# Four modulation chunks of the second layer moved between output projection tiles, attention scores handled map by map, and the order at the router changed

## What is computed

```python
def trunk_layer(x, cond, p, l, ctx_kv, ang):
    mod = cond @ p['w_mod'] + p['b_mod']                   # (1024) @ (1024, 6144)
    sh1, sc1, g1, sh2, sc2, g2 = jnp.split(mod[:, None, :], 6, axis=-1)
    h = rms_norm(x, p['g_pre_mix']) * (1.0 + sc1) + sh1
    y, k, v = mixer(h, p, l, ctx_kv, ang)                  # convolution, Hyena, differential attention, @ w_out
    x = x + g1 * rms_norm(y, p['g_post_mix'])
    h = rms_norm(x, p['g_pre_ffn']) * (1.0 + sc2) + sh2
    y = moe(h.reshape(B * L, D), p).reshape(B, L, D)       # sigmoid router, 64 experts, top 8, one shared expert
    return x + g2 * rms_norm(y, p['g_post_ffn']), k, v

    def block(qi):                                         # attention: two maps (c = 0, 1) for each head
        s = jnp.einsum('bhqcd,bhkcd->cbhqk', qi, k32) * scale
        pr = jax.nn.softmax(s, axis=-1)
        return jnp.einsum('bhqk,bhkd->bhqd', pr[0] - lam * pr[1], v32)
```

## Time and profile before

| | before |
|---|---|
| median of 3 runs | 1786.36 us (1785.29 to 1787.12) |
| the profiled execution | 1788.74 us, of which the span of the trace is 1786.9 us |
| mean granted TensorE clock | 0.974 |
| PE busy | 1687.2 us (94%) |
| DVE, ACT, POOL busy | 617.0 us (35%), 364.6 us (20%), 189.6 us (11%) |
| HBM read | 533.76 MB |

### The profile page before, as it was taken

How to read it: one execution, slowest core, us unless ns; L and a number is a source line. 1 busy time by engine, 2 the same in 40 slices (tenths; PEclk the granted TensorE clock), 3 DMA queues, 4 the chain that set the end, 5 groups by cost and what they waited for, 6 DMA issues and landing times.

```text
span 1786.9 us, 21952 instructions
## 1 busy us (share of the span) xinstructions
PE 1687.2 (94%) x8340; PEld 811.3 (45%) x8340; DVE 617.0 (35%) x1651; ACT 364.6 (20%) x820; POOL 189.6 (11%) x205
## 2 busy tenths in 40 slices
PE   4999889989999999999969998999999999999996
PEld 1555445544444444444435553555444444444442
DVE  2358362422222222222144674533222222222223
ACT  2110243211111111111141014431111111111111
POOL 0000000011111111111100000001111111111110
PEclk8999989999999999999979999899999999999998
DMA  9212690299999999999832138116799999999993
GB/s 402 97 78 94 244 378 2 70 381 368 418 401 412 417 392 415 420 419 419 350 130 94 63 127 335 54 47 275 307 414 419 397 421 392 411 419 420 419 420 134
DMA packets 77290, 530.50 MB, mean 297 GB/s; under 512 B 10881, under 2 KB 14081, under 8 KB 21633
## 3 DMA queue, kind: packets, MB, share of 16 engines
q1 hardware_dynamic: 67392, 503.90, 69.0%
q0 software_dynamic: 9792, 25.18, 3.6%
HBM read 533.76 MB, written 5.77 MB: 302 GB/s over the span
## 4 chain that ended last, share of the span: by engine, by line
PE 90%; DVE 4%; DMA 3%; ACT 2%; issue 1%; SPq 0%; ACTq 0%; POOL 0%; DVEq 0%
PE PSB L874 30%; PE PSB L883 15%; PE PSB L866 7%; PE PSB L861 6%; PE PSB L928 6%; PE PSB L929 5%; PE PSB L829 4%; PE PSB L916 4%; DMA RING<-in_wmod 3%; PE PSB L901 1%; PE PSB L649 1%; PE PSB L890 1%; PE PSB L781 1%; PE PSB L734 1%; PE PSB L719 1%
## 5 line engine op out<-in xcount | busy, mean ns | idle before, releaser
L874 PE MATMUL PSB<-WB,EX 128*32 128x512 f32 (+2 forms) x1408 | 431.9, 597 | 0.0
L874 PE MATMUL PSB<-RING,EX 128*32 128x512 f32 (+2 forms) x1344 | 417.1, 598 | 1.8 <-DVE EX L1667 1.8
L883 PE MATMUL PSB<-RING,AT 128*32 128x512 f32 (+2 forms) x720 | 229.9, 602 | 4.9 <-issue 3.8
L1685 DVE TENSOR_TENSOR YL<-PSB,YH 128x512 fp32r<-128x512 f32 x136 | 94.1, 692 | 357.2 <-ACT YH L1298 357.2
L883 PE MATMUL PSB<-WB,AT 128*32 128x512 f32 (+2 forms) x704 | 210.8, 596 | 0.0
L874 PEld LDWEIGHTS PSB<-WB,EX 128*32 128x32 f32 (+2 forms) x1408 | 113.3, 126 | 135.4 <-issue 135.3
L928 PE MATMUL PSB<-YH,SCAT 128*128 128x512 f32 x408 | 171.6, 421 | 2.8 <-DVE YL L1685 2.8
L537 POOL TENSOR_SCALAR SCAT<-CST,LSTT 128x384 fp32r<-128x384 f32 x68 | 84.9, 1249 | 836.6 <-PE PSB L929 836.4
L874 PEld LDWEIGHTS PSB<-RING,EX 128*32 128x32 f32 (+2 forms) x1344 | 105.8, 124 | 122.4 <-issue 122.4
L929 PE MATMUL PSB<-YL,SCAT 128*128 128x512 f32 x408 | 161.1, 395 | 0.0
L1667 DVE COPY EX<-PSB 128x512 f32<-128x512 f32 x68 | 47.0, 692 | 317.4 <-PE PSB L916 317.4
(11 more groups left out here) (265 smaller groups left out, 1708.5 us busy)
## 6 DMA issues: line engine op xcount, KB each, us to landing
RING<-in_exp_w_gate SPq DMA_DIRECT2D x64, 1024.0 KB, 12.5
RING<-in_exp_w_up SPq DMA_DIRECT2D x64, 1024.0 KB, 14.8
RING<-in_exp_w_down SPq DMA_DIRECT2D x64, 1024.0 KB, 13.3
WB<-in_exp_w_gate SPq DMA_DIRECT2D x64, 1024.0 KB, 10.3
WB<-in_exp_w_up SPq DMA_DIRECT2D x64, 1024.0 KB, 13.6
WB<-in_exp_w_down SPq DMA_DIRECT2D x64, 1024.0 KB, 13.5
RING<-in_wmod SPq DMA_DIRECT2D x16, 2048.0 KB, 10.6
KSYS<-in_wmod SPq DMA_DIRECT2D x8, 2048.0 KB, 11.5
```

The costliest lines, as they stand in the source:

```text
L874: mm = nc.tensor.matmul(PS[6][s0:s0 + w, :].rearrange("p (w f) -> p w f", w=2), e[:, k, s0:s0 + w], rawgu[n % NBUF][:, k], start=(k == 0), ...
L883: mm = nc.tensor.matmul(dst[s0:s0 + w, :], AT[:, j, s0:s0 + w], rawdn[n % NBUF][:, hf, j], start=(j == 0), stop=(j == 1))
L1685: v.tensor_tensor(YLb[s % 2][:, hf * 512:(hf + 1) * 512], PS[6 + hf][:, :], YHb[s % 2][:, hf * 512:(hf + 1) * 512].bitcast(F32), ALU.subtr ...
```

## The change

1. **Chunks 12 to 15** leave layer 0's attention. The attention loops of both layers now have the same filler (eight chunks, then pieces 0 to 6). Chunks 12 to 15 are multiplied between the `w_out` tiles, `mod_columns(2)` stands behind `router(0, 1)`; they use PS[4] and PS[5], and `to_features(l, 1, t)` takes the banks of its tile's `w_out` instead of PS[4] and PS[5]. SP issues chunks 12 to 15 behind the attention's loads, ACT's `mod_rows(2)` and `mod_column(2)` move along.
2. **Map by map:** the scores of each map signal and wait for themselves; DVE takes two reductions and two scalings where it took one each.
3. **At the router,** both layers: `shared_up(l, 0)` is cut in two halves with `to_features(l, 1, 2)` between them; ACT and DVE write the features of tile 2 ahead of the shared activations; DVE does `shared(l, 2)` ahead of the second list; `shared_down(l, 2, 0)` stands ahead of the wait for the third list.

```diff
...
         XNK = [x.rearrange("p t (q k) -> p t k q", k=KD) for x in XN]
-        FTB = ((0, 2, 4), (4, 4, 4))
+        FTB = ((0, 2, 4), (6, 0, 2))
+        ROWB = (6, 6, 4, 6)
+        COLB = (6, 5, 4, 5)
         YB = ((6, 0, 2), (0, 2, 4))
...
-            first, n = (4, 12) if l == 0 else (16, 8)
-            ended = {8: 1, 12: 2} if l == 0 else {8: 3}
-            return first + i if i < n else None, ended.get(i)
+            first = 4 if l == 0 else 16
+            return first + i if i < 8 else None, 2 * l + 1 if i == 8 else None
         def pieces(l, i):
-            if l == 0:
-                return range(0, 2) if i == 12 else range(2, 4) if i == 13 else range(0)
             return range(i - 9, i - 8) if 9 <= i < 12 else range(3, 5) if i == 12 else range(5, 7) if i == 13 else range(0)
...
                         weight_in(l, "o1")
+                if l == 0:
+                    for j in range(12, 16):
+                        mod_in(j)
                 sp.wait_ge(mod_used, 15 if l == 0 else 23)
...
-            def shared_up(l, t):
-
-                if t == 0:
+            def shared_up(l, t, first=0, last=KD):
+
+                if t == 0 and first == 0:
                     pe.wait_ge(gu_in[0], 32 * loads(l, 0))
-                for k in range(KD):
+                for k in range(first, last):
                     mm = gate_up(SHARED, HT[:, :, t * P:(t + 1) * P], k)
-                mm.then_inc(sh_gu, 1)
+                if last == KD:
+                    mm.then_inc(sh_gu, 1)
...
                 pe.wait_ge(d_sel, l + 1)
+                pe.wait_ge(a_col, 3)
                 for a in range(NT):
...
                 lists(l, 2)
+                shared_down(l, 2, 0)
                 pe.wait_ge(d_lst, LSTN * (NU * l + 3))
-                shared_down(l, 2, 0)
                 rows(l, 0, 0)
...
                         k0, kn = keys(t)
-                        if i >= 1:
-                            pe.wait_ge(a_exp, 2 * (NUN * l + i))
                         for c in range(2):
-                            mm = nc.tensor.matmul(PS[c][:, 0:kn * P],
-                                                  QT[c * DK:(c + 1) * DK, h, t * P:(t + 1) * P],
-                                                  KT[c * DK:(c + 1) * DK, h, k0:k0 + kn * P], start=True, stop=True)
-                        mm.then_inc(pe_S, 1)
+                            if i >= 1:
+                                pe.wait_ge(a_exp, 2 * (NUN * l + i - 1) + c + 1)
+                            nc.tensor.matmul(PS[c][:, 0:kn * P],
+                                             QT[c * DK:(c + 1) * DK, h, t * P:(t + 1) * P],
+                                             KT[c * DK:(c + 1) * DK, h, k0:k0 + kn * P], start=True, stop=True).then_inc(pe_S, 1)
                     if 1 <= i <= NUN:
...
                 gate_rows(l, 0, 0)
-                for p in range(4 if l == 0 else 7, 8):
+                for p in range(7, 8):
                     w_out_piece(l, p)
                 gate_rows(l, 0, 1)
                 pe.wait_ge(a_OT, NUN * (l + 1))
                 w_out(l, 1, 0)
+                if l == 0:
+                    mod_chunk(12)
                 w_out(l, 1, 1)
+                if l == 0:
+                    mod_chunk(13)
                 to_features(l, 1, 0)
                 pe.wait_ge(a_grow, 8 * l + 4)
                 w_out(l, 2, 0)
                 to_tokens(l, 0)
+                if l == 0:
+                    mod_chunk(14)
                 w_out(l, 2, 1)
+                if l == 0:
+                    mod_chunk(15)
                 to_features(l, 1, 1)
                 router(l, 0)
                 to_tokens(l, 1)
                 router(l, 1)
-                shared_up(l, 0)
+                if l == 0:
+                    mod_columns(2)
+                shared_up(l, 0, 0, 4)
                 to_features(l, 1, 2)
+                shared_up(l, 0, 4, KD)
                 router(l, 2)
...
                         kn = keys(units[i][0])[1]
-                        act.wait_ge(d_max, 2 * (NUN * l + i + 1))
                         if i >= 2:
                             act.wait_ge(d_P, K_P * l + 4 * (i - 1))
                         for c in range(2):
+                            act.wait_ge(d_max, 4 * (NUN * l + i) + 2 * c + 2)
                             own.sig(sc.activation(EX[:, i % 2, c, 0:kn * P], PS[c][:, 0:kn * P], ACT.Exp,
                                                   bias=ST[:, 46 + 2 * (i % 2) + c:47 + 2 * (i % 2) + c], scale=DK ** -0.5,
                                                   accum_out=ST[:, 50 + 2 * (i % 2) + c:51 + 2 * (i % 2) + c]), a_exp)
                     j, g = fill(l, i)
                     if g is not None:
                         mod_column(g)
-                    if j is not None and j + 1 in (12, 16, 24):
+                    if j is not None and j + 1 in (12, 24):
                         mod_rows(GROUP[j // 2])
...
                 features(l, 1, 1)
+                if l == 0:
+                    mod_rows(2)
                 tokens(l, 1)
                 squares(l, 1, 2)
+                if l == 0:
+                    mod_column(2)
+                features(l, 1, 2)
                 shared_sig(l, 0)
-                features(l, 1, 2)
                 act.wait_ge(pe_rt, l + 1)
...
                 lst(l, 0)
+                shared(l, 2)
                 onehot(l, 2)
                 lst(l, 1)
-                shared(l, 2)
                 lst(l, 2)
...
                         b = i % 2
-                        dve.wait_ge(pe_S, NUN * l + i + 1)
-                        do(v.tensor_reduce(ST[:, 42 + 2 * b:44 + 2 * b],
-                                           PSB[:, 0:1024].rearrange("p (c n) -> p c n", c=2)[:, :, 0:kn * P], AX, ALU.max), d_max)
-                        do(v.tensor_scalar(ST[:, 46 + 2 * b:48 + 2 * b], ST[:, 42 + 2 * b:44 + 2 * b], -(DK ** -0.5), None, ALU.mult), d_max)
+                        for c in range(2):
+                            m0 = 42 + 2 * b + c
+                            dve.wait_ge(pe_S, 2 * (NUN * l + i) + c + 1)
+                            do(v.tensor_reduce(ST[:, m0:m0 + 1], PS[c][:, 0:kn * P], AX, ALU.max), d_max)
+                            do(v.tensor_scalar(ST[:, m0 + 4:m0 + 5], ST[:, m0:m0 + 1], -(DK ** -0.5), None, ALU.mult), d_max)
                     if i >= 2:
...
                 normalise(l, 1, 2)
+                features(l, 1, 2)
                 shared(l, 0)
-                features(l, 1, 2)
                 mixture_dve(l)
...
```

8 lines of the change are left out of this document (4 added, 4 removed).

## The result

| | before | changed |
|---|---|---|
| median | 1786.74 us (1784.6 to 1790.89, 6 runs) | 1776.97 us (1772.31 to 1779.94, 6 runs) |
| profiled execution, its span | 1788.74, 1786.9 us | 1777.66, 1775.8 us |
| mean granted TensorE clock | 0.974 | 0.979 |

The ratio of the changed kernel's time to the time before is 0.9936, interval 0.9921 to 0.9951. The forecast was 1779.2 us (1775.3 to 1784.8): the sign and the range held, and the gain is 9.8 us by the medians, 11.1 us by the spans of the two profiles and 11.4 us by the ratio, where 7.2 was forecast.

The account below looks back on a forecast made before the run. The prediction took TensorE, 90% of the last-ending chain, as the bound. Its terms, -9.08 + 9.25 + 0.8 - 3.75 - 1.56 + 0 - 2.83 = -7.2 us, gave 1779.2 us from a median of 1786.36 us; range 1775.3 to 1784.8 us.

Parts of the forecast that it names:

- Chunks out of the attention: Layer 0's attention from i = 8 to the whole w_out tiles falls to layer 1's time, -9.08 us.
- The same chunks between the tiles: Between layer 0's w_out tiles, four chunks and mod_columns(2) add their full time, with loads in time, +9.25 us.
- Map by map: In both attention loops, two reductions and scalings cost DVE more, +0.8 us: +0.5 in layer 0, +0.3 in layer 1.
- The rival of the dear split: In attention, all 24 units pay 0.40 us for split maxima, 9.6 instead of 0.8 us; 1788.0 us, chance 0.06.
- `shared_up` in halves: Before the third router product, half of shared_up covers TensorE's wait for HT in both layers, -3.75 us.
- the first rival: The clock drop at layer 0's router stays or turns up elsewhere; -4.3 us, 1782.0 us, chance 0.25.
- Shared activations ahead of the second list: Behind the router, shared_flip(l, 2) waits for LSTW alone and starts 0.78 us earlier in each layer, -1.56 us.
- `shared_down` ahead of the third list's wait: The 1.90 us hole before shared_down(l, 2, 0) stays, since the product also waits for the GROW copies; 0 us.
- The slow stretch at the router: From layer 0's third router product to the counting matmuls, the clock stays up without the wait before it, -2.83 us.
- the first step: Layer 0's attention from i = 8 to the whole w_out tiles, without chunks 12 to 15, -9.08 us.
- the fourth in layer 0: shared_up to the third router product in layer 0: the wait for HT is covered, -1.88 us there.
- 3 to 4 us given back: Rival: layer 0's loop keeps some holes, or half the router gain returns as waits; about 1783.4 us, chance 0.10.

Follow-up runs that it names:

- the one reduction: The changed kernel with one reduction and one scaling for both maps, as before the change; 1776.0 us, ratio 0.9929.
- the whole `shared_up`: The changed kernel with shared_up(l, 0) in one piece ahead of to_features(l, 1, 2), ACT and DVE in their former order there; 1788.88 us, ratio 1.0003.
- the list order: The changed kernel with shared activations of tile 2 behind the second list and shared_down(l, 2, 0) behind the third list's wait again; 1781.3 us, ratio 0.9965.
- the columns alone: The changed kernel with mod_columns(2) behind the first half of shared_up(0, 0) instead of ahead of it; 1776.84 us, ratio 0.9928.
- the gate rows alone: The changed kernel with the second copy of the last gate rows (GROW) made by DVE beside ACT's first; 1773.57 us, ratio 0.9931.
- the two-engine copy: The changed kernel with the last gate rows (GROW) copied by ACT and DVE at once, instead of by ACT in turn; 1773.57 us, ratio 0.9931.
- the two attention edits: The changed kernel with late_norm spread over five units in smaller pieces and one reduction over both maps; 1764.62 us, ratio 0.9874.

## Why the prediction was right, and where it was off

- **Chunks out of the attention** (forecast -9.08, measured -13.24 us): mis-sized, because neither end of the subtraction was at full clock. The step took layer 1's 34.61 us (clock 0.85) from layer 0's 43.69 us (clock 0.92); the profiled changed kernel had 30.45 us at 1.00. So the price row held 4.2 us (34.61 - 30.45) of low clock that I took for work and holes, and the 43.69 us held about 3.3 us (estimate above), which was not there afterwards. At full clock the step is about -10 us. What the sum lacked is therefore the draw of the clock, and -13.24 us is in part luck: the repeat of the changed kernel had 33.30 us (0.90), which gives -10.4 us. In nine profiles with this filler and the old `late_norm` (before, the changed kernel twice, and the experiments on the chunks, the one reduction, the whole `shared_up`, the list order, the columns alone and the gate rows alone) layer 1 took 34.55 to 34.70 us four times and 31.83 to 31.98 us five times, and never 30.45. I had read the clock of the router, not of my price list.
- **The same chunks between the tiles** (+9.25, +9.47): right, with every load in time. The product behind a chunk is 0.1 us longer (7.13 instead of 7.03 us), and the transposes too (1.16 instead of 1.05 us). `mod_columns(2)` was priced by its busy 1.85 us; from start to start it took 1.70 us before and 1.76 us now. The sentence "the move alone wins nothing" is off by 2 to 2.6 us as measured, and by about 0.5 to 1.1 us at full clock.
- **Map by map** (+0.8, +1.02 in the profiled pair, 1.3 to 1.6 at equal clock): the sign is right, the size too small by 0.5 to 0.8 us, far from either bound. The waits behind i = 6 and 7 grew from 1.91 and 0.64 us to 2.48 and 0.97 us in layer 0, and the one behind i = 4, where `late_norm`'s first part stands and the step had put nothing, from 1.14 to 1.44 us. The rival of the dear split fell: it wanted +9.6 us. The rule of the Trainium skill weighed there ("VectorE: DVE Perf Modes", Rules for kernel authors: fewer DVE operations rather than fewer semaphores) has the right sign: the one reduction is faster by 1.3 to 1.6 us.
- **`shared_up` in halves** (-3.75): 2.0 us gone in each layer (9.85 to 7.84 us in layer 0 of the repeat, to 7.80 us in layer 1), but in the first profile layer 0's first half took 1.7 us longer at a clock of 0.68. That is the first rival, a drop that turns up elsewhere; the repeat had none there.
- **Shared activations ahead of the second list** (-1.56, -1.77): right, confirmed by its own experiment.
- **`shared_down` ahead of the third list's wait** (0, 0): right, and the reason (the GROW copies) is shown by the two-engine copy.
- **The slow stretch at the router** (-2.83, -2.91): right, and worth more than its term. The sum priced one drop in one profile. Putting the hole back cost 10 to 12 us, of which the rows explain 4.1 us by the hole itself; the rest goes with a lower clock, of which two drops are in sight. Which layer's stretch was slow was chance: in the kernel before it was layer 0's, with the hole put back layer 1's.
- **The Trainium skill's rule** that was weighed there ("TensorE: Matmul & The Clock Gate", What's actually happening: how many products run slow varies from run to run) would have left these 2.83 us out. Both hold: which stretch is slow is drawn anew in each execution, as the repeats show, but 0 of 24 against 2 of 4 at one place, and 28.5 to 48.1 us lost over whole kernels, are hardly one distribution (by single runs 42.8 to 51.8 us with the hole put back, 21.1 to 37.1 us with the two attention edits). The order of the work sets the odds.

Together: -4.2 us on the first step, +1.6 on the fourth in layer 0, -0.9 us in the start (the same program there) and -0.4 in small ones lead from the forecast -7.2 us to the -11.1 us of the spans. That the time came out within 2.2 us of the forecast owes something to luck, since the two large errors have opposite signs. One number of the rivals is a slip: with 3 to 4 us given back the sum gives 1782.2 to 1783.2 us, not 1783.4.
